# Moving blocks from two queues, and modulation tiles as the stationary operand of TensorE

## What is computed

```python
sh1, sc1, g1, sh2, sc2, g2 = jnp.split((silu_c @ w_mod[i] + b_mod[i])[:, None, :], N_MOD, axis=-1)
h_lat = modulate(rms_norm(x, norm_g[i, 0]), sh1, sc1)          # h * (1 + scale) + shift
x = x + g1 * rms_norm(fourier_mix(h_lat) @ fnet_w_out[slot], norm_g[i, 1])
x = x + g2 * rms_norm(sqrelu_mlp(modulate(rms_norm(x, norm_g[i, 2]), sh2, sc2), w_mlp_in[i], w_mlp_out[i]), norm_g[i, 3])
# second block: x + mixed_attention(rmsnorm(x)) @ w_out, then x + relu(h2 @ w_up)**2 @ w_down, then rmsnorm
```

## Time and profile before

| | |
|---|---|
| median of 3 runs | 2096.24 us (2095.48 to 2098.69) |
| the profiled execution | 2097.93 us, span of its records 2096.1 us |
| TensorE busy | 2027.7 us (97%) |
| VectorE busy | 1282.9 us (61%) |
| ScalarE busy | 1037.1 us (49%) |
| mean granted TensorE clock | 0.987 |
| DMA traffic | 484 MB, mean 231 GB/s |

### The profile page before, as it was taken

One profiled execution on the slowest core, in us unless ns is written; L12 is line 12 of the kernel. 1 busy time (PEld: TensorE's weight loads), 2 busy tenths in 40 slices (PEclk: granted clock), 3 DMA queues, 4 the chain that ended last, 5 costly groups with the idle time before them and its releaser, 6 DMA issues.

```text
span 2096.1 us, 23100 instructions
## 1 busy us (share of the span) xinstructions
PE 2027.7 (97%) x8885; PEld 1644.1 (78%) x8885; DVE 1282.9 (61%) x1313; ACT 1037.1 (49%) x1369; POOL 18.7 (1%) x23
## 2 busy tenths in 40 slices
PE   3999889999999999999999999999999999999998
PEld 1777568788888888887788888888888888888887
DVE  7989776656665555556556656655555555554555
ACT  3334434544444444544666755555444544544554
POOL 0000010000000000000000000000000000000000
PEclk9899889999999999999999999999999999999999
DMA  9999996877776666665556455466666665756663
GB/s 400 398 399 374 339 346 213 322 242 246 279 247 190 205 216 192 200 229 170 171 174 203 155 176 203 167 191 213 217 189 191 228 200 183 240 196 199 206 216 120
DMA packets 228854, 484.39 MB, mean 231 GB/s; under 512 B 17648, under 2 KB 38576, under 8 KB 219920
## 3 DMA queue, kind: packets, MB, share of 16 engines
q1 hardware_dynamic: 226768, 475.86, 66.3%
q0 software_dynamic: 816, 3.66, 0.5%
q10 hardware_dynamic: 1168, 3.46, 0.4%
HBM read 459.84 MB, written 2.10 MB: 220 GB/s over the span
## 4 chain that ended last, share of the span: by engine, by line
PE 82%; DVE 7%; DMA 6%; SPq 2%; ACT 2%; issue 1%; ACTq 0%; DVEq 0%
PE ps L524 26%; PE ps L526 26%; PE ps L525 26%; DVE scr L1388 3%; DVE w_low L1376 2%; DMA raw<-in_fnet_w 2%; DMA raw<-in_w_mod 2%; SPq L381 2%; DMA raw<-in_w_mlp_in 1%; PE ps L579 1%; ACT w_high L958 1%; PE ps L616 1%; DVE scr L1403 1%; DMA raw<-in_w_mlp_out 1%; PE ps L592 0%
## 5 line engine op out<-in xcount | busy, mean ns | idle before, releaser
L1376 DVE TENSOR_TENSOR w_low<-raw,w_high 128x1024 fp32r<-128x1024 f32 x672 | 816.9, 1222 | 675.9 <-ACT w_high L958 675.6
L958 ACT ACTIVATE w_high<-raw 128x1024 fp32r<-128x1024 f32 x672 | 705.7, 1058 | 860.0 <-PE ps L526 729.7
L524 PE MATMUL ps<-w_high,h_both 128*128 128x512 f32 x1536 | 607.8, 396 | 12.8 <-DVE w_low L1376 7.1
L525 PE MATMUL ps<-w_low,h_both 128*128 128x512 f32 x1536 | 600.9, 391 | 0.0
L526 PE MATMUL ps<-w_high,h_both 128*128 128x512 f32 x1536 | 600.8, 391 | 0.0
L524 PE MATMUL ps<-w_high,u_high 128*128 128x512 f32 x1152 | 449.8, 390 | 4.4 <-DVE w_low L1376 3.7
L526 PE MATMUL ps<-w_high,u_low 128*128 128x512 f32 x1152 | 448.3, 389 | 0.0
L525 PE MATMUL ps<-w_low,u_high 128*128 128x512 f32 x1152 | 448.2, 389 | 0.0
L524 PEld LDWEIGHTS ps<-w_high,h_both 128*128 128x128 f32 x1536 | 290.3, 189 | 77.8 <-issue 7.9
L526 PEld LDWEIGHTS ps<-w_high,h_both 128*128 128x128 f32 x1536 | 290.1, 189 | 61.4
L525 PEld LDWEIGHTS ps<-w_low,h_both 128*128 128x128 f32 x1536 | 290.5, 189 | 60.5 <-issue 1.4
(11 more groups left out here) (191 smaller groups left out, 811.9 us busy)
## 6 DMA issues: line engine op xcount, KB each, us to landing
raw<-in_w_mod SPq DMA_DIRECT2D x96, 1024.0 KB, 7.5
raw<-in_w_mlp_in SPq DMA_DIRECT2D x64, 1024.0 KB, 6.0
raw<-in_w_mlp_out SPq DMA_DIRECT2D x64, 1024.0 KB, 5.8
raw<-in_w_up SPq DMA_DIRECT2D x64, 1024.0 KB, 5.5
raw<-in_w_down SPq DMA_DIRECT2D x64, 1024.0 KB, 5.2
raw<-in_w_in SPq DMA_DIRECT2D x48, 1024.0 KB, 5.2
raw<-in_fnet_w SPq DMA_DIRECT2D x16, 1024.0 KB, 7.1
extra<-scr SPq DMA_DIRECT2D x512, 32.0 KB, 1.9
```

Of the source, the lines that this page charges most:

```text
L524: eng.matmul(dst, ah, wh, start=(k == 0), stop=False)
L525: eng.matmul(dst, ah, wl, start=False, stop=False)
L958: eng.activation(w_high[:, h % LEAD, :], raw[:, slot, (h % 2) * 2 * CW:(h % 2 + 1) * 2 * CW], ACT.Copy).then_inc(high_ready, 1)
L1376: eng.tensor_tensor(w_low[:, h % LEAD, :], raw[:, slot, piece], w_high[:, h % LEAD, :].bitcast(f32), ALU.subtract).then_inc(raw_used if h ...
```

## The change

It has two parts. **Moves shared:** in the first MLP and for queries and keys, SyncE issues 8 of the 16 moves of an exchange and GpSimd the other 8, on a semaphore of its own; the takers wait for both. The second MLP stays as it was. **Tiles as stationary operand:** a row on TensorE is now 16 matmuls instead of four; the 128x128 pieces of the weight tile are stationary, and the silu column is the one moving column. Results are columns of PSUM bank 6. The bias matmuls and `silu_p` go. DVE adds the columns of the four rows with a reduction of 128 x 8 x 4 values (`tile_columns`) after its row 6, and adds them to the sums in `mod_columns`; DVE's row 4 no longer waits for TensorE.

```diff
                 n = AT[unit, r]
                 eng.wait_ge(raw_loaded[n % RAW], 16 * (n // RAW + 1))
-                for k in range(2):
-                    weights = silu_p[:, 2 * r + k:2 * r + k + 1].to_broadcast([P, P])
-                    for j in range(2):
-                        column = k * HALF + j * CW
-                        last = eng.matmul(ps[:, ROW_BANK + j, :], weights, raw[:, n % RAW, column:column + CW],
-                                          start=False, stop=k == 1 and r == ROWS_ON_PE - 1)
+                for j in range(HALVES):
+                    at = TILE_COLUMN + r * HALVES + j
+                    for k in range(2):
+                        last = eng.matmul(ps[:, TILE_BANK, at:at + 1],
+                                          raw[:, n % RAW, k * HALF + j * P:k * HALF + (j + 1) * P],
+                                          silu_c[:, 2 * r + k:2 * r + k + 1], start=k == 0, stop=k == 1)
                 last.then_inc(raw_used_pe, 1)
-            def bias_rows(unit):
-
-                eng.wait_ge(acc_init[MOD_INIT.index(SC2A if unit == SC2A else SH2A)], 16)
-                for j in range(2):
-                    eng.matmul(ps[:, ROW_BANK + j, :], ident[0:1, :], mod_acc(unit)[0:1, j * CW:(j + 1) * CW],
-                               start=True, stop=False)
...
-                    if unit in (SC2A, SH2B) and r == ROWS_ON_PE and k == 0:
-                        eng.wait_ge(raw_used_pe, ROWS_ON_PE * (1 if unit == SC2A else 2))
-                        other = ps[:, ROW_BANK:ROW_BANK + 2, :].rearrange("p b n -> p (b n)")
...
+            def tile_columns(unit):
+
+                eng.wait_ge(raw_used_pe, ROWS_ON_PE * (1 if unit == SC2A else 2))
+                parts = ps[:, TILE_BANK, TILE_COLUMN:TILE_COLUMN + TILE_COLUMNS]
+                own = slice(0, HALVES) if unit == SC2A else slice(HALVES, KT)
+                link(eng.tensor_reduce(tile_sums[:, own], parts.rearrange("p (r j) -> p j r", r=ROWS_ON_PE),
+                                       AX.X, ALU.add))
...
+                if v == SC2A:
+                    link(eng.tensor_tensor(tile_sums[:, at], src, tile_sums[:, at], ALU.add))
+                    src = tile_sums[:, at]
...
-                for a in range(QUADS):
+                for a in groups:
                     for q in range(QUADS):
                         eng.dma_start(exchanged[q * BLOCK:(q + 1) * BLOCK, a * RUN:(a + 1) * RUN],
                                       blocks[a * BLOCK:(a + 1) * BLOCK, q * RUN:(q + 1) * RUN])\
                            .then_inc(t_exchanged[c % 2], 16)
...
-                        exchange(c)
+                        exchange(c, SYNC_GROUPS)
...
+            for n in range(QUARTERS * NC):
+                eng.wait_ge(t_blocks, n + 1)
+                for a in POOL_GROUPS:
+                    for q in range(QUADS):
+                        eng.dma_start(exchanged[q * BLOCK:(q + 1) * BLOCK, a * RUN:(a + 1) * RUN],
+                                      blocks[a * BLOCK:(a + 1) * BLOCK, q * RUN:(q + 1) * RUN])\
+                           .then_inc(t_exchanged_pool[n % 2], 16)
...
+                if shared:
+                    eng.wait_ge(t_exchanged[c % 2], SHARE * (c // 2 + 1) + earlier)
+                    eng.wait_ge(t_exchanged_pool[c % 2], SHARE * (c // 2 + 1) + earlier)
```

More of the change, by code:

```diff
@@ L373, in first_chunk, with exchange @@
                 mlp_chunk(w_mlp_in, w_mlp_out, 0, QUARTER_CHUNKS.index((c, j)))
-            def exchange(c):
+            def exchange(c, groups=range(QUADS)):
                 t.add("blocks")
                 eng.wait_ge(t_blocks, t.at("blocks", 0))
-                for a in range(QUADS):
+                for a in groups:
                     for q in range(QUADS):
@@ L383, in exchange, with exchange_behind @@
                            .then_inc(t_exchanged[c % 2], 16)
-            def exchange_behind(ch):
+            def exchange_behind(ch, groups=range(QUADS)):
                 for c, y in enumerate(UP_ENDS):
                     if ch == y // 2 + EXCHANGED_BEHIND:
-                        exchange(c)
+                        exchange(c, groups)
             for n, (unit, k) in enumerate(FRONT):
@@ L432, in exchange_qk @@
                     eng.wait_ge(a_turned, TT * m)
-                for a in range(QUADS):
+                for a in SYNC_GROUPS:
                     for q in range(QUADS):
@@ L494, in _ @@
                 eng.dma_start(bf[:, tt * HEADS:(tt + 1) * HEADS], b_f.broadcast_to([P, HEADS])).then_inc(f_raw, 16)
+            for n in range(QUARTERS * NC):
[5 more added lines that the diff above has]
+                           .then_inc(t_exchanged_pool[n % 2], 16)
+            for m in range(2 * GROUPS):
+                eng.wait_ge(a_blocks, m + 1)
+                if m:
+                    eng.wait_ge(a_turned, TT * m)
+                for a in POOL_GROUPS:
+                    for q in range(QUADS):
+                        eng.dma_start(qk_moved[q * BLOCK:(q + 1) * BLOCK, a * RUN:(a + 1) * RUN],
+                                      stage[a * BLOCK:(a + 1) * BLOCK, q * RUN:(q + 1) * RUN])\
+                           .then_inc(a_exchanged_pool, 16)
             eng.wait_ge(o_ready, GROUPS * GH)
@@ L743, in _ @@
             norm_turn(6, 8)
-            last_read(SC2A, ROWS_ON_PE)
-            bias_rows(SH2B)
             eng.wait_ge(b_copied, 4)
@@ L1079, in mlp_body @@
                     if y in TAKES:
-                        take_exchanged(TAKES[y], t.at("moved", 0))
+                        take_exchanged(TAKES[y], t.at("moved", 0), not scaled)
                     if hh == 7:
@@ L1397, in half_tile @@
                 sums = mod_acc(unit)
+                if unit == SC2A and r == ROWS_ON_PE:
+                    eng.wait_ge(acc_init[MOD_INIT.index(SC2A)], 16)
                 for k in range(2):
-                    other = sums
-                    if unit in (SC2A, SH2B) and r == ROWS_ON_PE and k == 0:
-                        eng.wait_ge(raw_used_pe, ROWS_ON_PE * (1 if unit == SC2A else 2))
-                        other = ps[:, ROW_BANK:ROW_BANK + 2, :].rearrange("p b n -> p (b n)")
                     ins = eng.scalar_tensor_tensor(out=sums, in0=raw[:, slot, k * HALF:(k + 1) * HALF],
-                                                   scalar=silu_c[:, 2 * r + k:2 * r + k + 1], in1=other,
+                                                   scalar=silu_c[:, 2 * r + k:2 * r + k + 1], in1=sums,
                                                    op0=ALU.mult, op1=ALU.add)
@@ L1424, in mod_columns @@
                     eng.tensor_scalar(shift1[:, :], src, float(SEQ), None, ALU.mult).then_inc(mod_cols, 1)
-                else:
-                    eng.tensor_copy(mcol[:, 2 * KT:3 * KT][:, at], src).then_inc(mod_cols, 1)
+                elif v == SH2A:
+                    eng.tensor_copy(mcol[:, 2 * KT:3 * KT][:, at], src).then_inc(mod_cols, 1)
+                else:
+                    eng.tensor_tensor(mcol[:, 2 * KT:3 * KT][:, at], src, tile_sums[:, at], ALU.add)\
+                       .then_inc(mod_cols, 1)
             def add_shift():
@@ L1675, in _ @@
                 front_tile(n)
+                if n == AT[SC2A, 6]:
+                    tile_columns(SC2A)
+                elif n == AT[SH2B, 6]:
+                    tile_columns(SH2B)
                 if n == AT[SH2A, 6]:
```

34 lines of the change are left out of this document (19 added, 15 removed).

## The result

| | before | changed |
|---|---|---|
| median (13 executions each, same chip) | 2098.34 us (2093.42 to 2105.21) | 2103.45 us (2100.06 to 2106.54) |
| span of the profiled execution | 2096.1 us | 2100.7 us |
| mean granted TensorE clock | 0.987 | 0.981 |

The ratio is 1.0025, with a 95% interval from 1.0017 to 1.0032: slower by 5.1 us (3.6 to 6.7). The forecast was 2102.6 us and slower. One profiled execution took 2102.52 us, so its trace stands for the median. Beside the later experiments the kernel before was timed again on two further chips, at 2099.63 us (9 executions) and 2099.15 us (25); one of the nine took 3701.87 us at a granted clock of 0.74 and is in no comparison.

What follows compares the result with a forecast made beforehand. It took TensorE as full from 420 to 2088 us and the order of waits as deciding from 200 to 310 us. Front +9 and moves -2.6 summed to +6.4 us, median 2102.6 us, range 2092.5 to 2110.

Steps and rivals of the forecast that it cites:

- The operand alone costs nothing: TensorE's eight tiles: at the same clock the new form costs 3.5 us a tile against 3.43, 0.07 us more.
- The clock: Four SC2A tiles and SH2A sums: clock falls to half 3.2 us into 72 one-column matmuls, which end at 234.8 us.
- rival A: Tiles on TensorE: gap-free work holds the clock, sum about -4 us, time 2092.2 us; 15% chance.
- The way on: From tiles to UP: DVE's delayed copy and queued rows make DVE some 9 us late, TensorE 8 to 11.4.
- +9 to the end of the front: End of the front: the first UP tile's delay carries through unchanged 12 us steps, +9 us (bounds +6 and +13).
- the SH2B rows are covered: SH2B rows 1 to 3 on TensorE: 3.4 us more each at half clock, hidden by up to 12 us idle.
- Rival B: Front: clock falls late or loads catch up, +3 to +6 us, time 2096 to 2100 us; 13% chance.
- The moves, -2.6: Shared moves: weight loads leave 5 us earlier, closing TensorE's 2.63 us gap at 372.27; -2.6 us (bounds 0 and -2.6).
- their cover at 10.9 us: ACT's exchange waits: delay reaches TensorE only past four halves of lead, about 10.9 us at 12 x 0.227 a half.
- GpSimd at nothing: GpSimd's eight moves: 4 to 9.5 us issue plus 2 to 6 us after the blocks, covered, taken at 0.
- Rival C: GpSimd's moves come late at 15.5 us, ACT waits 3.6 us more in 16 exchanges; 2107 to 2130 us, 7% chance.
- The sum: Whole kernel: +9 - 2.6 = +6.4 us, profiled execution 2104.3 us, median 2102.6 us.

Runs made afterwards that it cites:

- wide: Changed kernel, but every tile matmul moves the silu column repeated into 128 equal columns; 2091.77 us, 0.9960 of the kernel before (timed again: 2092.99 us, 0.9970).
- moves_only: Kernel before with the moves shared by SyncE and GpSimd, tiles in the old form with bias matmuls; 2092.43 us, 0.9963 of the kernel before.
- copy_later: Changed kernel, but DVE copies the SH2A sums behind rows 5 to 7 of SC2A instead of ahead; 2105.38 us, 1.0037 of the kernel before.
- tiles_only: Kernel before with the tiles as stationary operand, SyncE still issuing all 16 moves; 2109.41 us, 1.0048 of the kernel before.
- wide_sc2a: Changed kernel, but only the four SC2A rows move 128 equal columns, the SH2B rows keep one; 2091.24 us, 0.9961 of the kernel before.
- wide_sums: As wide, and the sums over partitions also move 128 columns of ones instead of one; 2091.83 us, 0.9967 of the kernel before.
- pool_all: Kernel before, old tiles, GpSimd issuing all 16 moves of each exchange in the first MLP and for queries and keys; 2099.05 us, 1.0003 of before.

## Why the prediction was right

**The operand alone costs nothing: right.** At full clock a tile is 3.63 us against 3.43, and wide equals moves_only within the intervals (0.9960, 0.9963). They differ in the form of the tiles and in what goes with it, the bias matmuls and DVE's additions.

**The clock: right, and the heart of it.** It fell 4.1 us into the run (at 211; I had 3.2, bounds 1.5 and 5). The run ended at 234.40, against 234.8. The step was carried over from the earlier trace rows, where the same shape did the same, and wide shows by experiment that the column count does it. The fall at 59.9 us was weaker ground than I took it for: after the same 16 sums the clock held in five of nine traces, the changed kernel's among them. The run of 72 lost it in three traces of three, so the step held. The Trainium skill, "TensorE: Matmul & The Clock Gate", section "Why this matters for your kernels", names idle gaps as what lowers the clock and continuous work as what keeps it up. Here 20.00 busy of 20.00 us ran at 0.50, and wide, with more idle time, at 1.00, so page and measurement differ and the measurement decides; rival A, which went by that rule, is out.

**The way on: right in place.** Copy at 234.64 (234.9), row 7 done at 242.8 (243.1), sums at 242.95 (243.4), scale at 245.19 (246 to 247), UP at 251.25 ("near 251"). copy_later adds to this: DVE's path and the path of TensorE and the slots were nearly equal, so neither alone was the cause.

**+9 to the end of the front: right, as closely as one trace can tell.** 10.1 in the changed kernel, 7.6 in tiles_only. Two traces of one kernel lie 4.6 apart, so the closeness is partly luck; the ratio of tiles_only gives 10.1 us (7.1 to 13.2). That the SH2B rows are covered is confirmed by wide_sc2a. Rival B had +3 to +6 and a time up to 2100 us.

**The moves, -2.6: right in mechanism, too small.** The gap of the earlier trace rows closed, and for the reason given: ACT's wait for the load behind the moves went from 9.22 to 4.19 us. The rest of the program gained 5.4 us (4.6 in moves_only). Of it 2.6 are this gap and 1.05 the one at 547.80 us. That second gap is where the prediction was wrong: it took ACT's waits of up to 7.3 us for `extra` as covered and put their cover at 10.9 us, but TensorE had a gap behind 7.3 us. Another 1.2 us (1.0 in moves_only) are clock, not moves: behind the `mcol` row half clock lasts until 320.1 us in the changed kernel, 6.4 us, and until 312.5 after a `mcol` row at 303.69 before, 8.8 us. In wide_sums, with shared moves, it lasts 9.1 us, so this part is scatter. With that 4.9 of the 5.4 us and all of the 4.6 are placed. The ratio of moves_only gives the sharing 7.8 us, at least 4.8, which is more than its trace shows; 1.7 us of it are that the profiled execution of the kernel before was faster than the median beside moves_only, and the rest stays open. The Trainium skill, "DMA: Bandwidth & Descriptors", section "Issuing engines are not separate DMA queues", holds that several issuing engines save only a usually small issue time. Here issue was 10 us against 1.9 us of landing, and the saving was real: many small moves are not the usual case.

**GpSimd at nothing: right for eight moves.** 3.9 us and 3.0 of landing, at the low end of what I allowed (4 to 9.5 and 2 to 6). SyncE's own landing rose from 2.0 to 3.3 us beside it, which I had not counted and which did no harm. Rival C, late moves, is what pool_all shows with 16.

**The sum.** +10.1 and -5.4 in place of +9 and -2.6, with the clock's own end 0.4 us early: two errors of opposite sign left 4.7 where I had 6.4. The median was 0.85 us off, partly because the medians of the kernel before moved too, from 2096.24 to 2098.34 us. Against that one the difference is 5.1.

## What to carry to other kernels

Before turning a long matmul into many one-column ones, look for such a run in the trace of before and read the granted clock behind it; if it falls there, price the run at half clock. A short run that keeps the clock in one trace proves little, as the 16 sums at 55 us show, so look at more than one. Where one column is all that is needed, 128 equal columns cost 0.1 us more for 16 matmuls and here saved 3.1 us a tile by keeping the clock. Many small moves are worth splitting over two issuing engines where a taker waits for the last of them or for a load that is issued behind them; giving all of them to the other engine trades the second wait for the first.

## What was not expected of the hardware

- A matmul of 128 moving columns takes hardly longer than one of a single column when each has a new 128x128 float32 stationary piece: 3.73 us against 3.63 for 16, both at full clock. In wide the weight loads are busy for 14.31 of the 15.10 us, which points to them as what sets the pace.
- A run of 64 of them holds the clock at 1.00 with 128 columns, in spite of 0.60 us of idle time, and falls to 0.50 with one column, with 0.19 us.
- GpSimd issues a 32 KB move in 0.49 us, where SyncE takes 0.62 to 0.72; landing grows from 3.0 us with eight of them in a row to 4.3 with sixteen. SyncE's moves land in 2.0 us alone and in 3.3 beside GpSimd's.
- The same 16 one-column sums lost the clock in four traces and kept it in five, with no idle time in any of them.
- The front of one and the same kernel took 94.7 us in one execution and 99.3 in another, where the second tile's load came 2.57 us late instead of 0.60. That is nearly half of the effect studied.
